# Residual added by TensorE in the experts' down banks, one expert loaded further ahead, and four idle products before the first gather: one-core decoder trunk

## What is computed

```python
for layer in range(2):
    mix = even_mixer(h, ...) if layer % 2 == 0 else odd_mixer(h, ...)
    h = layer_norm(ALPHA * h + mix, ln_g[layer, 0], ln_b[layer, 0])
    ffn = moe_ffn(h, router_w, router_bias, w_gate[layer], w_up[layer], w_down[layer])
    h = layer_norm(ALPHA * h + ffn, ln_g[layer, 1], ln_b[layer, 1])

# moe_ffn: every token goes to 2 of 32 experts; the two gates of a token sum to 1
expert(x, e) = (silu(x @ w_gate[e]) * (x @ w_up[e])) @ w_down[e]    # 1024 -> 256 -> 1024
out[token] = sum over its 2 experts of gate * expert(x[token], e)
```

## Time and profile before

| | |
|---|---|
| median of 3 runs | 1185.07 us (1183.59 to 1186.3) |
| time of the profiled execution | 1183.87 us |
| its span in the profile | 1182.1 us |
| TensorE busy, mean granted clock | 1026.6 us (87%), 0.957 of full speed |
| VectorE, ScalarE busy | 496.6 us (42%), 292.1 us (25%) |
| transfers | 284.85 MB, 241 GB/s on average |
| chain that ended last | PE 65%, DMA 14%, DVE 7%, SPq 7%, issue 4%, ACT 3% |

### The profile page before, as it was taken

The page is one execution under the profiler, slowest core; times in us unless marked ns, Lnnn a source line. Parts: engine busy times, 40 slices in busy tenths (PEclk is TensorE's granted clock), DMA queues, the critical chain, the costliest instruction groups (busy, mean ns, idle before and its releaser), DMA issues.

```text
span 1182.1 us, 14606 instructions
## 1 busy us (share of the span) xinstructions
PE 1026.6 (87%) x5590; PEld 678.1 (57%) x5590; DVE 496.6 (42%) x1269; ACT 292.1 (25%) x508; POOL 107.7 (9%) x161
## 2 busy tenths in 40 slices
PE   7999999998388878876899999999984888788863
PEld 6878888887233323332498987888871343243321
DVE  3862575556623211113756444426566232121118
ACT  3343223223111111213222332323331122122110
POOL 5000000000202111111000000000002111111110
PEclk8989999999699999999999999999996999999987
DMA  8345333287679999996522422221495899999944
GB/s 210 101 72 107 72 72 107 72 317 292 254 319 420 424 425 423 426 424 259 214 72 72 143 72 72 73 72 37 190 372 217 349 424 423 424 424 425 424 170 175
DMA packets 73158, 284.85 MB, mean 241 GB/s; under 512 B 10940, under 2 KB 27340, under 8 KB 47488
## 3 DMA queue, kind: packets, MB, share of 16 engines
q1 hardware_dynamic: 57520, 234.90, 52.6%
q10 hardware_dynamic: 4896, 31.46, 6.4%
q0 software_dynamic: 10672, 17.55, 4.2%
HBM read 280.72 MB, written 23.07 MB: 257 GB/s over the span
## 4 chain that ended last, share of the span: by engine, by line
PE 65%; DMA 14%; DVE 7%; SPq 7%; issue 4%; ACT 3%; ACTq 0%; POOLq 0%; DVEq 0%; POOL 0%
PE bank L1691 15%; PE bank L2018 14%; PE bank L1893 12%; DMA wgu<-in_w_up 11%; PE bank L1916 5%; SPq L440 4%; SPq L445 2%; PE bank L2053 2%; PE bank L1709 2%; PE bank L1882 2%; PE bank L2086 2%; PE bank L1795 2%; PE bank L1780 1%; PE bank L1718 1%; PE bank L1985 1%
## 5 line engine op out<-in xcount | busy, mean ns | idle before, releaser
L1893 PE MATMUL bank<-wgu,xgt 128*64 128x512 f32 x1024 | 235.7, 613 | 22.8 <-DMA wgu<-in_w_up 19.3
L1893 PEld LDWEIGHTS bank<-wgu,xgt 128*64 128x64 f32 x1024 | 86.6, 142 | 167.2 <-issue 155.2
L1916 PE MATMUL bank<-wd,htt 128*64 128x512 f32 x496 | 116.8, 597 | 50.0 <-issue 48.4
L984 DVE TENSOR_TENSOR wl<-raw,wh 128x2048 fp32r<-128x2048 f32 x37 | 84.8, 2291 | 133.6 <-ACT wh L684 133.5
L684 ACT ACTIVATE wh<-raw 128x2048 fp32r<-128x2048 f32 x37 | 70.8, 1913 | 154.9 <-PE bank L1691 99.7
L1372 DVE TENSOR_TENSOR hh<-sg,bank 128x256 f32<-128x256 f32 x32 | 13.5, 421 | 225.3 <-ACT sg L839 225.3
L1916 PEld LDWEIGHTS bank<-wd,htt 128*64 128x64 f32 x496 | 39.8, 136 | 104.5 <-issue 104.5
L1377 DVE COPY yt<-bank 128x512 f32<-128x512 f32 x32 | 22.1, 691 | 135.2 <-PE bank L1916 135.2
L831 ACT ACTIVATE xgt<-bank,lnt 128x128 f32<-128x128 f32 x136 | 51.1, 456 | 67.5 <-PE bank L1882 67.5
L839 ACT ACTIVATE sg<-bank 128x256 f32<-128x256 f32 x32 | 12.3, 384 | 215.7 <-PE bank L1893 215.7
L2018 PE MATMUL bank<-xt_hi,wh 128*128 128x512 f32 x160 | 63.4, 397 | 0.6 <-DVE qg L1504 0.6
(11 more groups left out here) (352 smaller groups left out, 1715.1 us busy)
## 6 DMA issues: line engine op xcount, KB each, us to landing
wgu<-in_w_gate SPq DMA_DIRECT2D x64, 1024.0 KB, 20.2
wgu<-in_w_up SPq DMA_DIRECT2D x64, 1024.0 KB, 22.8
wd<-in_w_down SPq DMA_DIRECT2D x36, 1024.0 KB, 24.6
wd<-in_w_down ACTq DMA_DIRECT2D x26, 1024.0 KB, 10.3
raw<-in_w_in_even SPq DMA_DIRECT2D x15, 1024.0 KB, 7.9
raw<-in_w_in_odd SPq DMA_DIRECT2D x28, 512.0 KB, 4.4
y<-y_rows SPq DMA_DIRECT2D x8, 1024.0 KB, 8.4
h<-in_x SPq DMA_DIRECT2D x8, 512.0 KB, 4.9
```

Source lines behind the costliest of these rows:

```text
L984: dve.tensor_tensor(wl[slot][:, :, :], raw_of(u, slot)[:, :, :], wh[slot][:, :, :], ALU.subtract)\
L1893: ins = pe.matmul(bank[2][B * b:B * (b + 1), :], xgt[:, k, B * b:B * (b + 1)], wgu[s][:, b, :, k, :], start=(k == 0), stop=(k == KT - 1))
L1916: ins = pe.matmul(bank[5 + n][B * b:B * (b + 1), :], htt[:, k, B * b:B * (b + 1)], w[:, n * 512:(n + 1) * 512], start=(k == 0), stop=(k == 1))
```

## The change

- The residual moves from after the experts to inside each pair. `residual(q)` stands between `hidden_t(q)` and `down(q)`: 16 products, each with one 128 x 128 tile of `xgt` as the stationary operand and 64 columns of ALPHA times the identity (`aident`) as the moving one, written to every eighth column of banks 5 and 6. `down` then adds to these banks. The 8 VectorE operations, the 4 identity products of each layer, `lnab` and its loads, and `h_scaled` go.
- `xgt` is held twice, so `keep_rows` no longer waits for `gate_up`; ScalarE copies `htt` ahead of `keep_rows`.
- In the places set free expert 6 is held apart from the slots, too: `wdx[0]` (where `lnab` was) for its down weights, `wgx` (where h is) for its gate and up weights. SP issues these 3 MB before the weights of pair 3, of which only 2 MB are left to issue then.
- `keep_warm(4)` stands behind the tables' product (L1873), ahead of the first turned rows.

The core of the diff:

```diff
-        lnab = Zone(4 * KB, 8 * KB).take("lnab", [P, 2, D], f32)
+        spare = Zone(4 * KB, 12 * KB)
+        wdx = [spare.take("wdx0", [P, 2, D], f32)]
+        xgt = [spare.take("xgt1", [P, KT, P], f32)]
...
+        aident = Zone(const.at, KB).take("aident", [P, P], f32)
...
+        wgx = Zone(BASE + 18 * KB, 16 * KB).take("wgx", [P, 2, KT, F], f32)
...
+
+                def down(e):
+                    sp.dma_start(wdx[e - 6][:, :, :].rearrange("p k n -> p (k n)"),
+                                 w_down[l][e:e + 1].rearrange("a (p k) n -> p (a k n)", p=P)).then_inc(wdx_in[l], 16)
+
+                down(6)
+                sp.wait_ge(rows_out, 16 * NT * (l + 1))
+                sp.wait_ge(rt_ps, NT * (l + 1))
+                for i, w in enumerate((w_gate, w_up)):
+                    sp.dma_start(wgx[:, i, :, :].rearrange("p k f -> p (k f)"),
+                                 w[l][6:7].rearrange("a (p k) f -> p (a k f)", p=P)).then_inc(wgx_in[l], 16)
                 sp.wait_ge(xg_in[l][2], 16)
-                sp.dma_start(wdx[:, :, :].rearrange("p k n -> p (k n)"),
-                             w_down[l][7:8].rearrange("a (p k) n -> p (a k n)", p=P)).then_inc(wdx_in[l], 16)
+                down(7)
...
                 for q in range(3, NFIX):
                     sp.wait_ge(gu_done[l], q - 2)
-                    load_gate_up(l, q % 3, (2 * q, 2 * q + 1))
+                    if q == 3:
+                        load_gate_up(l, 0, (7,), at=1)
+                    else:
+                        load_gate_up(l, q % 3, (2 * q, 2 * q + 1))
...
@@ -531,7 +540,7 @@
             load_pair(1, 2, (4, 5))
             sp.wait_ge(unit_done, U_WOUT2 + 2 + 2)
...
-                def keep_rows(q):
+                def keep_rows(q, par):
                     act.wait_ge(xg_tr[l], q + 1)
-                    if not isinstance(q, int) or q:
-                        act.wait_ge(gu_done[l], q)
                     for k in range(4):
-                        ins = act.activation(xgt[:, k, :], bank[0][:, k * P:(k + 1) * P], ACT.Identity,
+                        ins = act.activation(xgt[par][:, k, :], bank[0][:, k * P:(k + 1) * P], ACT.Identity,
                                              scale=lnt[:, l, 0, k:k + 1], bias=lnt[:, l, 1, k:k + 1])
                     ins.then_inc(xgt_a[l], 1)
 
@@ -837,24 +844,24 @@
...
                         act.wait_ge(hh_ready[l], q)
                     act.activation(sg[:, :], bank[2][:, 0:F], ACT.Silu).then_inc(sg_ready[l], 1)
-                    keep_rows(q + 1)
                     act.wait_ge(ht_tr[l], q + 1)
                     if not first:
                         act.wait_ge(dn_done[l], q)
                     act.activation(htt[:, :, :], bank[4][:, 0:2 * P].rearrange("p (k t) -> p k t", t=P),
                                    ACT.Copy).then_inc(ht_sb[l], 1)
+                    keep_rows(q + 1, 1 - par)
                     act.wait_ge(dn_done[l], q + 1)
...
                 for q in range(NFIX):
                     pair(q, q % 2, q == 0)
-                    if q + 3 < NFIX:
+                    if 0 < q < NFIX - 3:
                         s = q % 3
-                        for b in range(2 if q else 1):
+                        for b in range(2):
                             act.dma_start(wd[s][:, b, :, :].rearrange("p k n -> p (k n)"),
                                           w_down[l][2 * (q + 3) + b:2 * (q + 3) + b + 1]
...
                         dve.wait_ge(y_out[l][q % 2], 16 * (q // 2))
                     keep_y(q % 2)
-                    if 1 <= q <= NT:
-                        t = q - 1
-                        dve.wait_ge(rows_out, 16 * NT * (l + 1))
-                        dve.wait_ge(ln_in, 32 * (2 * l + 1))
-                        link(dve.scalar_tensor_tensor(h[:, t, :], h[:, t, :], ALPHA, lnab[:, 0, :], ALU.mult, ALU.mult))
-                        ins = dve.scalar_tensor_tensor(h[:, t, :], lnab[:, 1, :], ALPHA, h[:, t, :], ALU.mult, ALU.add)
-                        if q == NT:
-                            ins.then_inc(h_scaled, 1)
                 iters = dve.value_load(ni[0:1, 0:1], min_val=1, max_val=3)
                 with dve.Fori(0, iters) as it:
...
                 dve.wait_ge(y2_in[t], 16 * (l + 1))
-                for c in range(2):
-                    link(dve.scalar_tensor_tensor(hs, y2[t][:, c * D:c * D + C], ga[:, c, t:t + 1], hs, ALU.mult, ALU.add))
+                link(dve.tensor_scalar(hs, y2[t][:, 0:C], ga[:, 0, t:t + 1], None, ALU.mult))
+                link(dve.scalar_tensor_tensor(hs, y2[t][:, D:D + C], ga[:, 1, t:t + 1], hs, ALU.mult, ALU.add))
                 tile_stats(t, 0)
...
+            dve.tensor_scalar(aident[:, :], ident[:, :], ALPHA, None, ALU.mult).then_inc(aident_ready, 1)
...
                                     start=(c == 0), stop=(c == 7))
                 ins.then_inc(tb_ps, 1)
+                keep_warm(4)
...
-                            ins = pe.matmul(bank[2][B * b:B * (b + 1), :], xgt[:, k, B * b:B * (b + 1)],
-                                            wgu[s][:, b, :, k, :], start=(k == 0), stop=(k == KT - 1))
+                            w = wgx[:, :, k, :] if extra and not b else wgu[s][:, b, :, k, :]
+                            ins = pe.matmul(bank[2][B * b:B * (b + 1), :], xgt[par][:, k, B * b:B * (b + 1)],
+                                            w, start=(k == 0), stop=(k == KT - 1))
...
-                def down(q, s, first, extra=False):
-                    pe.wait_ge(ht_sb[l], q + 1)
+                def residual(q, par, first):
                     if first:
                         pe.wait_ge(tb_ready, l + 1)
+                        pe.wait_ge(aident_ready, 1)
                     else:
                         pe.wait_ge(ya_ready[l], q)
                         pe.wait_ge(yd_ready[l], q)
+                    for k in range(KT):
+                        for n in range(2):
+                            pe.matmul(bank[5 + n][:, k:512:KT], xgt[par][:, k, :], aident[:, 64 * n:64 * (n + 1)],
+                                      start=(k == 0), stop=False)
+
+                def down(q, s, extra=False):
+                    pe.wait_ge(ht_sb[l], q + 1)
                     for n in range(2):
                         for k in range(2):
                             for b in range(2):
-                                w = wdx[:, k, :] if extra and b else wd[s][:, b, k, :]
+                                w = wdx[b][:, k, :] if extra else wd[s][:, b, k, :]
                                 ins = pe.matmul(bank[5 + n][B * b:B * (b + 1), :], htt[:, k, B * b:B * (b + 1)],
-                                                w[:, n * 512:(n + 1) * 512],
-                                                start=(k == 0), stop=(k == 1))
+                                                w[:, n * 512:(n + 1) * 512], start=False, stop=(k == 1))
...
-                    gate_up(q, s, q == 0)
+                    pe.wait_ge(wgu_in[l][s], 64 * (q // 3 + 1) - (32 if q >= 3 and s == 0 else 0))
+                    if q == 3:
+                        pe.wait_ge(wgx_in[l], 32)
+                    gate_up(q, s, q % 2, q == 0, q == 3)
...
-                    pe.wait_ge(wd_in[l][s], 32 * (q // 3 + 1) - (16 if q >= 3 and s == 0 else 0))
+                    residual(q, q % 2, q == 0)
                     if q == 3:
-                        pe.wait_ge(wdx_in[l], 16)
-                    down(q, s, q == 0, q == 3)
+                        pe.wait_ge(wdx_in[l], 32)
+                    else:
+                        pe.wait_ge(wd_in[l][s], 32 * (q // 3 + (0 if q > 3 and s == 0 else 1)))
+                    down(q, s, q == 3)
...
-                pe.wait_ge(h_scaled, l + 1)
                 for t in range(NT):
                     pe.wait_ge(y2_in[t], 16 * (l + 1))
                     for c in range(2):
-                        pe.matmul(bank[4 + t][:, :], dga[:, t, c, :], y2[t][:, c * D + C:(c + 1) * D],
-                                  start=(c == 0), stop=False)
-                    pe.matmul(bank[4 + t][:, :], ident[:, :], h[:, t, C:D], start=False, stop=True).then_inc(right_ready, 1)
+                        ins = pe.matmul(bank[4 + t][:, :], dga[:, t, c, :], y2[t][:, c * D + C:(c + 1) * D],
+                                  start=(c == 0), stop=(c == 1))
+                    ins.then_inc(right_ready, 1)
```

More of the change, by code:

```diff
@@ L154, in trunk @@
         mbd = lngb_z.take("mbd", [P, NT, P], f32)
-        wdx = Zone(const.at, 8 * KB).take("wdx", [P, 2, D], f32)
+        wdx.append(Zone(const.at, 8 * KB).take("wdx1", [P, 2, D], f32))
         lngb = const.take("lngb", [P, 2, D], f32)
@@ L231, in trunk @@
         xg = [z.take(f"xg{i}", [P, D], f32) for i in range(3)]
-        xgt = z.take("xgt", [P, KT, P], f32)
+        xgt.insert(0, z.take("xgt0", [P, KT, P], f32))
         z = Zone(A + 16 * KB, 8 * KB)
@@ L340, in trunk @@
         wd_in = [[sem(f"down_in{l}{i}") for i in range(3)] for l in range(2)]
```

(28 more changed lines are left out.)

34 lines of the change are left out of this document (11 added, 23 removed).

## The result

The changed kernel takes 1207.12 us, the median of four runs (1205.75 to 1208.26), against 1184.33 (1182.12 to 1186.3) for the kernel before in the same measurement: a ratio of 1.0187 [1.0166, 1.0209]; in brackets stands the 95% interval of a ratio, here and below. The forecast was 1206, in a range of 1195 to 1219. The profiled execution took 1205.75 us.

A forecast was written before the change was run, and what follows sets the result against it. Transfers bound the experts' stages, TensorE close behind; the added products would make TensorE the limit. 1183.87 + 11.2 + 11.6 - 0.87 - 0.87 = 1204.9 us, plus 1.2 for the median: 1206, range 1195 to 1219.

The forecast's parts named there:

- The price of an added instruction: Added residual products in each pair: 32 instructions at 111 ns, the odd mixer's square product's price, 3.55 us.
- L1639's 64 ns: Transposes with 128 columns loaded and 5 streamed, 64 ns each; taken as lower bound of an added instruction's price.
- The slope of the loads: Loads of 32, 64, 128 columns: 0.75 to 0.86 ns a column, so 96 to 110 ns for 128.
- the second rival: Added products: loads don't overlap with streaming; 165 ns each, a pair 17.0 us, 1261 us in all. Chance 0.04.
- The pair: Experts' stages: hidden transposes to down take 3.80 us instead of 2.08, so a pair grows from 13.53 to 15.25 us.
- TensorE as the limit: Experts' stages: a pair of 15.25 us exceeds the transfers' 14.54, so TensorE sets the end of both stages.
- The first rival: Experts' stages: loads hide at 64 ns, a pair takes 13.75 us, transfers stay the limit; 1180 us. Chance 0.13.
- The start of the stages: Before the experts: idle products take 6.0 us, turned rows save 0.99; first products start at 323.0 and 911.0, full clock.
- Behind the stages: After the experts: identity product of each tile goes, -0.87 us in each layer; `add_left`'s saving counted at nothing.
- The expert held ahead: Weight transfers: 3 MB moved before `gate_up(0)`, worth 7.4 us a layer if the queue went on; counted at nothing.
- one sign that did not come: Weight queue: should fall idle some 5 us behind `gate_up(0)` and again later in the stage.
- The forecast case: Whole kernel: added instructions cost 100 to 124 ns, TensorE sets the end; 1206 us, between 1195 and 1219. Chance 0.80.

The follow-up runs named there:

- both other kinds of kernel: Changed kernel with eight products of 128 columns instead of sixteen of 64: 1175.68 us; changed kernel with no residual products at all: 1172.47 us.
- the same places with sixteen products: Changed kernel, its 16 products of 64 columns kept, weight places shifted by one expert from pair 4 on: 1208.84 us, 1.0199 of the kernel before.
- the places in another order: Changed kernel with 8 products of 128 columns and weight places shifted by one expert from pair 4 on: 1162.5 us, 0.9805 of the kernel before.
- wide products: Changed kernel with 8 products of 128 columns instead of 16 of 64: 1174.59 us run again; 1178.41 us without the expert held ahead.

## Why the prediction came out

The time is 1.1 us from the forecast, but not all of that closeness is earned. The terms, each by the prediction's own step:

**The price of an added instruction: right.** 111 ns taken, 110 measured, from the square product of the odd mixer. L1639's 64 ns was no guide. The slope of the loads was: half as many instructions, each with its load, took half the time, and halving the moving columns changed nothing. By the Trainium skill, TensorE: Matmul & The Clock Gate, section LDWEIGHTS (loading the stationary operand), a load takes its columns divided by 1.2 in ns, which is an estimate of 107 ns for 128 columns, and the 110 ns of the trace agree to 3. (What the prediction says with it on fast loading stands in the Trainium skill on the same page, section Weight-path perf modes — Fast Weight Load (FWL) and DoubleRow.) The 110 ns hold a load and the streaming together, which leaves no room for the second rival, whose price was 165. The Trainium skill, the same page, section The mechanism, says two things on such an overlap: that a load goes ahead of running products on other rows of the array or into a background weight buffer, and further down that it overlaps only on other rows. The prediction gave the second alone. These loads take all 128 rows, so the 110 ns speak against the second; they fit the background buffer, which no run shows by itself.

**The pair: right in kind, 0.16 us short.** 15.25 forecast, 15.41 measured. From the hidden transposes to the down products it was 3.80 by the sum and is 362.32 - 358.37 = 3.95: the products' run is the 3.5 that was said, and the two transposes with the handover to the next line take 0.43 rather than 0.25. I had timed two transposes as a quarter of the eight. Sixteen pairs, the last one 0.03 longer and the first products' 7.09 in place of 6.87 make 2.8 of the 3.1 us by which each stage is longer than the 244.0 of the sum; the pair with which the loop begins, 0.2 longer than the others, is most of the rest.

**TensorE as the limit: right.** The pair lies above 14.54, the waits for weights are gone, and both other kinds of kernel show the other side of the threshold: at 13.68 and 12.52 us a pair the transfers are back in the chain. The first rival's price was never seen, but its consequence was: with half the instructions the time is 1175.7, near its 1180.

**The start of the stages: right, and then some.** The idle products took 6.02 us (6.0 forecast), the turned rows 1.17 in the chain (0.99), the gather 4.71 (0.3 dearer, as counted), the first products 7.09 at full clock. But layer 0 starts at 319.53 and not at 323.0. Of these 3.5 us most lie in a stretch of the even mixer that the change doesn't touch. The windows of it, first the kernel before and then the changed one:

```profile
60.00:75.00 15.00, 15.00 (x60) 9.64 (x59) 11.31 (x16) 2.58 (x3) 1.28 (x1) 0.77 0.41 70
```

```profile
60.00:75.00 15.00, 15.00 (x73) 10.39 (x72) 14.31 (x19) 6.26 (x8) 1.29 (x1) 1.00 0.39 70
```

The first has the clock at 0.77 and gets 60 products done, the second 73: 3.3 us that the two executions differ by in code that is the same. Chance is the likely cause: the eleven other traces of the case, two of them of the kernel before, show this stretch at 0.77 or 0.89, the kernel that lacks only the idle products among them, and 1.00 was met once. I took the profiled execution's own time as the base without asking which of its stretches would come out otherwise.

**Behind the stages: too little counted.** From the end of layer 0's stage to the start of layer 1's it was 355.12 us and is 352.68: -2.44 where -0.87 and +0.06 were forecast. Of it 1.37 are the sixteen transposes that happened to run at full clock (3.41 to 2.04 us, 2.06 in the kernel before run again), so chance as well; the rest fits the identity product that went and VectorE's cheaper `add_left` (the two operations of a tile take 1.53 us before, 0.48 + 0.75 = 1.23 after), which the forecast counted at nothing. At the end it was -1.14 for -0.87.

**The expert held ahead: right at nothing in this change, with one sign that did not come.** Behind `gate_up(0)` the queue falls to 88 GB/s as the count of bytes said. But it does not fall idle again later in the stage: it is full from 344 to 530 us. TensorE still waits for no weights; the likely reason, which no run tests, is that it begins with three pairs and expert 6 loaded ahead. The reason why earlier weights give nothing holds (the same places with sixteen products gain nothing); where TensorE leaves room, the idea with the places in another order gives 12 us. In a kernel with wide products, counting it at nothing would have been 1 to 3 us a layer off.

So the balance of the two profiled spans, +21.8 us, is -4.2 before the first product (3.3 of it probably chance), +15.0 and +14.6 for the stages, -2.4 between them and -1.1 behind. The forecast's was +21.0. Step by step the measured time stands off the forecast by -3.5 us before the first product, +6.2 in the stages, -1.6 between them and -0.3 behind. The forecast case is shown: TensorE sets the end, and the added products cost 110 ns an instruction. That the number fell within 1.1 us of the median is in part luck, errors that cancel.

## What to carry to other kernels

A float32 product with a full stationary tile and few moving columns is priced by its load (32, 64 and 128 moving columns cost 109 to 113 ns an instruction here), so before moving an addition to TensorE count loads and not columns, and let each loaded tile stream more of them: here 16 products of 64 moving columns against 8 of 128 is the difference between 1.9% slower and 0.7% faster. Compare the sum with the pace of the second limit for the repeated unit (14.54 us against 15.25 and 13.68), since what stays below it hardly counts. And an extra buffer ahead of a loop buys most of its bytes' time only if the queue has a freed place to go on with, and nothing while TensorE sets the end.

## What the runs showed of the hardware beyond that

- The granted clock fell from 1.00 to 0.50 behind 32 back-to-back float32 loads and products with 32 moving columns, while TensorE never stood idle; the down products behind them took 813 ns apiece in place of 598, 47.5 us over the kernel. With 64 moving columns it stayed at 1.00 through the pair, and with 128 the down products kept their 598 ns. Which quantity decides isn't settled by these three sizes.
- Idle products before the first gather of a stage were worth 4.9 to 6.9 us in the changed kernel and 6.8 in the kernel before, though the stages of the latter are limited by transfers; the runs don't tell the two apart. How much of the 6.8 is the clock's chance elsewhere (1.4 us at the sixteen transposes in its profile) was not separated.
- Which stretches of the mixers run at the low clock changes between executions of the same kernel: one stretch of some 12 us differed by 1.6 us between the two traces of the kernel before, and by 3.3 between the kernel before and the changed one, whose code there is the same. A sum against one profiled execution has that much play before any step of it is wrong.
